# Convolution steps and one norm moved in the order of the first block's mixers

## The reference, cut to what matters

```python
z_a, z_b, z_c, z_d = _split(hn @ w_in[i], [A_COLS, B_COLS, C_COLS, D_COLS])
...
def conformer_conv(z, conv_w, conv_b, ln_g, ln_b):
    z1, z2 = jnp.split(z, 2, axis=-1)
    h = z1 * jax.nn.sigmoid(z2)
    h = causal_depthwise_conv(h, conv_w) + conv_b      # 31 taps
    h = layer_norm(h, ln_g, ln_b, LN_EPS)
    return jax.nn.silu(h)

def rwkv7_time_mix(P, mu, ...):
    P = P + (P_prev - P) * mu                          # r, k, v, and xw, xa, xg
    w = -jax.nn.softplus(-(w0 + jnp.tanh(xw) @ w2)) - 0.5
    a = jax.nn.sigmoid(a0 + xa @ a2)
    gate = jax.nn.sigmoid(xg) @ g2
    ...                                                # chunked recurrence
    y = y + jnp.sum(r_h * k_h * r_k, axis=-1, keepdims=True) * v_h
```

## Time and profile before

| | us |
|---|---|
| median of three runs (lowest, highest) | 3183.69 (3182.38, 3184.23) |
| the profiled execution's own time | 3183.69 |
| its span in the profile | 3181.4 |
| TensorE busy | 3073.9 (97% of the span) |
| VectorE busy | 1984.8 (62%) |
| ScalarE busy | 861.0 (27%) |
| GpSimd busy | 1345.7 (42%) |
| TensorE idle at L449, waiting for L1500 | 17.2 |
| TensorE idle at L672, waiting for L1480 | 7.6 |

### The profile page before, as it was taken

The page is one execution under the profiler, slowest core; times in us unless marked ns, Lnnn a source line. Parts: engine busy times, 40 slices in busy tenths (PEclk is TensorE's granted clock), DMA queues, the critical chain, the costliest instruction groups (busy, mean ns, idle before and its releaser), DMA issues.

```text
span 3181.4 us, 35229 instructions
## 1 busy us (share of the span) xinstructions
PE 3073.9 (97%) x13146; PEld 2078.0 (65%) x13146; DVE 1984.8 (62%) x2716; ACT 861.0 (27%) x1530; POOL 1345.7 (42%) x1016
## 2 busy tenths in 40 slices
PE   8998998999999999999999999999999999999997
PEld 3445563874578888788644544544555588888886
DVE  2386888653578788787526654753125665577876
ACT  3343334321233333100213335203223344410002
POOL 0010010002599999555411000351015798855555
PEclk9999999999999999999999999999999999999998
DMA  4211111152222222666212111212121233376652
GB/s 142 67 60 34 50 34 53 54 172 93 80 80 85 85 100 90 226 234 227 67 54 90 57 54 53 77 43 66 53 80 53 113 140 146 126 254 234 220 197 81
DMA packets 206279, 335.70 MB, mean 106 GB/s; under 512 B 10145, under 2 KB 123297, under 8 KB 205345
## 3 DMA queue, kind: packets, MB, share of 16 engines
q1 hardware_dynamic: 204688, 330.45, 29.9%
q10 hardware_dynamic: 1424, 3.02, 0.3%
HBM read 269.21 MB, written 64.23 MB: 105 GB/s over the span
## 4 chain that ended last, share of the span: by engine, by line
PE 82%; DVE 9%; POOL 4%; ACT 2%; issue 1%; DMA 1%; ACTq 0%; SPq 0%; DVEq 0%; POOLq 0%
PE psum L3627 21%; PE psum L3907 14%; PE psum L181 10%; PE psum L2680 8%; PE psum L407 7%; PE psum L2082 3%; PE psum L4474 3%; PE psum L3644 2%; PE psum L563 1%; DVE arena L1380 1%; DVE arena L1378 1%; PE psum L4451 1%; PE psum L4412 1%; PE psum L2088 1%; DVE arena L1480 1%
## 5 line engine op out<-in xcount | busy, mean ns | idle before, releaser
L3627 PE MATMUL psum<-arena 128*128 128x256 f32 x2632 | 598.0, 381 | 14.2 <-DVE arena L3672 7.4
L3907 PE MATMUL psum<-arena 128*128 128x256 f32 x2660 | 585.9, 383 | 10.2 <-POOL arena L3933 5.3
L3907 PEld LDWEIGHTS psum<-arena 128*128 128x128 f32 x2660 | 510.7, 192 | 84.0 <-POOL arena L3933 7.1
L3627 PEld LDWEIGHTS psum<-arena 128*128 128x128 f32 x2632 | 499.4, 191 | 93.6 <-DVE arena L3672 11.2
L407 PE MATMUL psum<-arena 128*128 128x512 f32 x768 | 337.6, 598 | 7.1 <-DVE arena L1236 4.9
L181 PE MATMUL psum<-arena 128*128 128x512 f32 x768 | 332.4, 592 | 1.5 <-ACT arena L4644 1.5
L407 PEld LDWEIGHTS psum<-arena 128*128 128x128 f32 x768 | 146.0, 192 | 189.5 <-issue 184.8
L181 PEld LDWEIGHTS psum<-arena 128*128 128x128 f32 x768 | 145.8, 190 | 182.1 <-issue 180.6
L2680 PE MATMUL psum<-arena 128*128 128x512 f32 x576 | 251.5, 595 | 0.0
L2680 PEld LDWEIGHTS psum<-arena 128*128 128x128 f32 x576 | 109.0, 191 | 136.4 <-issue 136.4
L2369 DVE TENSOR_TENSOR arena<-arena 128x1024 f32<-128x1024 f32 x77 | 144.3, 1874 | 33.6 <-ACT arena L3664 23.8
(11 more groups left out here) (540 smaller groups left out, 4830.7 us busy)
## 6 DMA issues: line engine op xcount, KB each, us to landing
arena<-w_in SPq DMA_DIRECT2D x42, 1024.0 KB, 5.3
arena<-mlp_w SPq DMA_DIRECT2D x72, 512.0 KB, 6.9
arena<-w_ffn_down SPq DMA_DIRECT2D x36, 512.0 KB, 6.8
arena<-mlp_w SPq DMA_DIRECT2D x8, 2048.0 KB, 8.6
mlp_hidden_T<-arena SPq DMA_DIRECT2D x32, 512.0 KB, 2.6
arena<-mlp_hidden_T SPq DMA_DIRECT2D x16, 1024.0 KB, 5.6
arena<-w_out SPq DMA_DIRECT2D x12, 1024.0 KB, 5.4
mlp_hidden_B<-arena SPq DMA_DIRECT2D x24, 512.0 KB, 2.6
```

The source lines that it names most:

```text
L3627: mm = self.env.nc.tensor.matmul(self.ps(n, m), left[:, k, :], right[:, k, :], start=(m in (1, 5, 2) and k == 0), stop=(k == 1), skip_grou ...
L3907: mm = self.env.nc.tensor.matmul(ps[:, 256 * r:256 * r + 256], left[:, s, r * P:(r + 1) * P], right[:, s, :], start=(first and s == 0 and ...
```

## The change

Only the order of work changes, in the stage's three programs for TensorE, ScalarE and VectorE; no instruction is added or taken away, apart from table loads of ScalarE that follow from its order.

- First half, VectorE: all 62 steps now stand before `dn_grams(0)`, as 25, 3, 3, 4, 8, 11 and 8, and `mix` is split by tile so that steps come between its two tiles. The 24 steps behind `conv("v", 1)` are gone, and none are left between `mix("rv", 2, 0)` and `dn_grams(0)`.
- Second half, VectorE: `mix("rx", 3, 1)` comes ahead of the last nine steps, and `layer("cf", 1)` goes from ahead of `prepare(1)` to behind `bonus(1)`.
- Second half, TensorE: the centring goes behind the dot products `dots(1)`, the variance behind `dn_norm(1)`.
- Second half, ScalarE: `layer` is cut into `layer_roots` and `layer_out`. `lora_in(1)` and `lora_out(1)` follow `mixes("rx", 3, 1)` directly; squares and root of the norm come behind `dn_squares(1)` with `rates(1)` between them, ahead of `dn_roots(1)`; the Silu comes behind `rw_grams(1)`.

```diff
@@ -764,11 +764,12 @@
             key_norm(1)
             next(low_rank)
             next(low_rank, None)
-            layer("cf", 1)
             lora(1)
             chunks("dn", 1)
             dots(1)
+            layer_centre("cf", 1)
             dn_norm(1)
+            layer_variance("cf", 1)
             memory("K", 0)
             rw_tokens(1)
             rw_grams(1)
@@ -996,7 +997,7 @@
                     tiles.wait(act, name, h, i)
                     tiles.take(A(dst(i), tiles.ps(name, h, i), ACT.Gelu_apprx_tanh), name, h, i)
 
-            def layer(name, h, behind_squares=None, behind_root=None, root=None):
+            def layer_roots(name, h, behind_squares=None, root=None):
                 for i in range(2):
                     key = ("centre", name, h, i)
                     tiles.wait(act, *key)
@@ -1007,8 +1008,8 @@
                     root()
                 else:
                     inverse_root(ln_sq[name][0], ("var", name, h), s["ln_rs"], 1.0 / 256, "eps5")
-                if behind_root:
-                    behind_root()
+
+            def layer_out(name, h):
                 for i in range(2):
                     tiles.wait_taken(act, "centre", name, h, i)
                     x = ln_src[name](i, h)
@@ -1017,6 +1018,10 @@
                     else:
                         ins = A(x, x, ACT.Silu, bias=env.col("cf_ln_b", i))
                     ins.then_inc(s["ln_out"], 1)
+
+            def layer(name, h, behind_squares=None, root=None):
+                layer_roots(name, h, behind_squares, root)
+                layer_out(name, h)
 
             def turned_values(h):
                 for j in range(2):
@@ -1208,14 +1213,16 @@
             mixes("rv", 2, 1)
             key_roots(1)
             mixes("rx", 3, 1)
-            layer("cf", 1, lambda: lora_in(1), lambda: lora_out(1))
+            lora_in(1)
+            lora_out(1)
             chunks("dn", 1)
             dn_squares(1)
-            rates(1)
+            layer_roots("cf", 1, lambda: rates(1))
             dn_roots(1)
             memory(0, 0)
             rw_tokens(1)
             rw_grams(1)
+            layer_out("cf", 1)
             for g in range(2, 4):
                 memory(0, g)
             for g in range(4):
@@ -1566,19 +1573,24 @@
             conv("q", 0)
             glu(0)
             taps = taps_of(0)
-            some(taps, 12)
+            some(taps, 25)
             dn_scalars(0)
-            mix("r", 0, 0)
+            mix("r", 0, 0, (0,))
+            some(taps, 3)
+            mix("r", 0, 0, (1,))
             values(0)
+            some(taps, 3)
             q_scale(0)
             some(taps, 4)
-            mix("rk", 1, 0)
+            mix("rk", 1, 0, (0,))
+            some(taps, 8)
+            mix("rk", 1, 0, (1,))
             dn_decays(0)
-            some(taps, 6)
-            mix("rv", 2, 0)
-            some(taps, 14)
+            some(taps, 11)
+            mix("rv", 2, 0, (0,))
+            some(taps, 8)
+            mix("rv", 2, 0, (1,))
             mix("rx", 3, 0)
-            some(taps, 2)
             dn_grams(0)
             some(inverse("dn", 0), BLOCK)
             layer("gm", 0)
@@ -1591,7 +1603,6 @@
             dn_final(0)
             decayed(0)
             conv("v", 1)
-            some(taps, 62)
             spread_out(0)
             rw_grams(0)
             steps = inverse("rw", 0)
@@ -1622,14 +1633,14 @@
             spread_out(1)
             some(taps, 9)
             mix("rv", 2, 1)
+            mix("rx", 3, 1)
             some(taps, 62)
-            mix("rx", 3, 1)
-            layer("cf", 1)
             prepare(1)
             solve("dn", 1)
             carry("dn", 1)
             sums(1)
             bonus(1)
+            layer("cf", 1)
             dn_final(1)
             decayed(1)
             rw_grams(1)
```

## The result

The changed kernel takes 3163.38 us, the median of 6 runs (3160.81 to 3165.11), beside 3183.96 for the kernel before (6 runs, 3182.38 to 3184.63). The ratio is 0.9935 with an interval of 0.9924 to 0.9945: 20.6 us faster, inside the range forecast and 4.4 us above the single value, which puts it beyond the upper end of the forecast's own band (3156.5 to 3161.5) and near the 3164 of rival (a). The profiled execution took 3161.91 us with a span of 3159.6.

The account below looks back on a forecast made before the run. TensorE, nearly always on the chain that ended last, was taken as the bound through its idle time; 17.6 + 14.2 - 6.8 = 25.0 us off 3183.69 gives 3158.7, say 3159, range 3153.5 to 3168.

Parts of the forecast that it names:

- rival (a): Second half: ScalarE's roots decide, early start worth only 10.2 us, all 8.3 us of delay on the path; 3164, chance 0.17.
- The front costs nothing: First half, ahead of the grams: 40 convolution steps of 0.67 us fit VectorE's waits, tightest with 0.3 us spare; 0 taken.
- rival (e): Front: added steps collide with GpSimd and slow to as much as 2.39 us each, time then 3212; chance 0.03.
- The back, 17.6: First half, `spread_out(0)`: starts 15.9 us earlier, plus 1.7 for the clock staying up; 17.6 us, between 14.9 and 20.1.
- Rival (d): First half: the first wait is only handed on to ScalarE's copies, so this half gives nothing; 3176, chance 0.05.
- The early start, 14.2: Second half: earlier rx mix and tanh let U start at 554.2 instead of 568.42; 14.2 us, bounds 10.2 and 15.8.
- rival (b): Second half: no slow clock in the low-rank products and roots hidden, 10.4 us from this half; 3156, chance 0.12.
- Given back, 6.8: Second half, behind the dot products: moved norm and later roots delay the grams by 6.8 us, between 5.4 and 8.3.
- (c): ScalarE's roots: a table switch holds it longer than the load, roots 2.6 us later if counted twice; 3161.3, chance 0.02.

Follow-up runs that it names:

- the block of 26: Changed kernel with the front's steps as before and the remaining 26 convolution steps in one block ahead of the grams: 3181.12 us, ratio 0.9990.
- The first half alone: Kernel before with only the 40 convolution steps spread over VectorE's waits and `spread_out(0)` straight behind `conv("v", 1)`: 3166.26 us, ratio 0.9949.
- the repeated run: The changed kernel itself, unaltered, measured again in a later group: 3161.29 us, ratio 0.9926.
- the norm alone: Changed kernel with the rx mix behind its nine convolution steps again, so the norm is moved but the low-rank inputs are not early: 3166.93 us, ratio 0.9949.
- the early inputs alone: Changed kernel with the second half's whole norm back in front of the delta rule, behind the low-rank products: 3164.10 us, ratio 0.9933.
- two table loads fewer: Changed kernel with the logarithms of the norm's and the delta rule's roots side by side, then both exponentials: 3160.45 us in one execution.
- the second half alone: Changed kernel with the front's steps and the block of 24 steps as in the kernel before: 3178.71 us, ratio 0.9986.

## Why the prediction was right

The sum was 17.6 + 14.2 - 6.8 = 25.0 us. The mixers of the profiled execution gave 499.08 - 477.42 = 21.7. Every part of the sum is there, and what is missing lies on one side: it was a little too good in three places.

- **The front costs nothing: right.** All gaps held, with 1.04, 1.21 and 0.39 us left in three of them. The steps stayed at 0.67 us, so rival (e) is out, and the block of 26 shows what the steps cost without the gaps.
- **The back, 17.6: right, at most 0.4 too large.** The first half alone gave 17.6 in the runs; 1.32 us of its wait are left where 1.3 was forecast, and the clock did not fall. In the traces, the changed kernel's and that of the first half alone, the end of the last projection comes 17.2 us earlier against the first low-rank products: 15.9 of wait, and 1.4 instead of 1.7 for the clock that no longer falls (from the start of the turn to the next projection 12.59 us for 13.98). Rival (d) is out.
- **The early start, 14.2: the mechanism right, the size 1.4 too large.** From the end of the last projection U was 568.42 - 528.08 = 40.34 us away, that end being the centring's start less its wait; now it is 537.67 - (503.07 + 7.03) = 27.57. That is 12.8 gained. The low-rank products started 5.9 us behind the projection, as forecast (5.8), at the lower clock, which rules out rival (b); but they and the hand-over to YT took 6.0 us, not 5.4, and from H to U it was 11.9, not 11.2, with a stall of 0.96 instead of 0.4: the preparation, after its first instruction, waited another 0.41 us for ScalarE's copy of a low-rank product.
- **Given back, 6.8: right, and by the path forecast.** Dot products to grams is 27.77 us now and 20.94 before, 6.8 more. What waits for the roots, `decayed` (L1563), starts 22.12 us behind the dot products instead of 13.88, 8.2 late where 8.3 was forecast. TensorE's queue has 5.48 us of norm more, where 5.4 was forecast, and `decayed` is what TensorE waits for last, 1.24 us where the sum had 0.8. What the sum did not say is that the roots are not alone: two table loads less on ScalarE moved the grams by 0.3 only, since the centring's bank is then late. Rival (a) is out: the roots were late, but what they cost is within that 1.24, and the early start is worth 12.8 and not the 10.2 of that rival. Each added load shows 1.28 us and the logarithm right behind it (563.34 and 564.64), so (c) is out too.
- **What was not in the sum: 1.5 us behind the grams.** From the grams to the first product behind the mixers it is 92.67 us instead of 91.19. The wait ahead of the last YT was 2.21 us before and 2.51 after; behind it the clock fell, and the products took 5.47 instead of 3.84. The prediction took a wait as short as 1.3 us as safe by the 2.36 of the earlier trace rows, which held, and did not look at this place, whose wait it left as it was. Nor is 2.36 the shortest wait with slow work behind it: the kernel before has one of 2.18 (503.48 above). In the repeated run of the same kernel the clock did not fall at the last YT, and the mixers took 476.00 instead of 477.42 us. What decides it is not shown by any run here.

So the mixers miss the sum by 3.3 us: 0.4 in the first half, 1.4 of early start, 1.5 behind the grams. The median run is another 1.5 above the profiled one, within the 4 us between this kernel's own runs. That the median lies near the 3164 of rival (a) does not speak for that rival: the trace contradicts both of its terms.

## What to carry to other kernels

Work that fills another engine's waits is free only gap by gap: count the room of each wait in the trace, and check that what stands behind the block is late anyway; the same 26 steps in one block cost 17 us. Where an early start has two causes that hold it, taking away one gains little and taking both is more than the sum (3.7, 6.2, together 12.8). And work that is moved off one path joins the queue of another: put it under a stretch that waits for nobody, and look what the removed wait was covering, since that is bare afterwards.

## What the runs showed of the hardware

A wait of 2.2 to 2.5 us ahead of the same 32 products left TensorE at full speed in some executions and at the lower clock in others, and its length did not decide which. The last YT took 3.84 us behind 2.21 (before), 2.27 (the norm alone), 2.29 (the early inputs alone), 2.31 (the repeated run), 2.47 (the first half alone) and 2.51 (two loads fewer), but 5.47 behind 2.27 (the second half alone), 2.47 (one block) and 2.51 (after): each of the last three lengths stands among the first ones too. What stood ahead of the wait was the same memory products in all of them. An estimate of such a place has to carry both prices, here 0 and 1.63 us.

The 32 projection products (L407) that start at 503.48 in the kernel before show the same. They take 15.70 us behind a wait of 2.18 there and of 2.22 after, and 14.00 behind 2.16 in the repeated run, whose row this is:

```profile
487.10 14.00 PE L407 MATMUL psum<-arena 128*128 128x512 f32 x32 [2.16 <-DVE arena L1288]
```

There the lower clock costs nothing: where these products were fast, TensorE waited 1.80 us for VectorE right behind them, and where they were slow it did not.
